# Seven block products for two chunks in every second round of an expert matmul, on one core

## The chip, the cores and the metric

The program runs on 1 core of one Trainium2 chip. The metric is the device time of one execution in microseconds (us); the kernel before has a median of 1713.93 us over 3 runs (1713.11 to 1713.99).

## The reference

Two transformer blocks in float32 on 256 tokens of width 1024. The part that matters is the PEER feed-forward of the first block: each token picks experts out of 16384, and the layer adds, for every picked expert e, g_e * gelu(u_e . x) * v_e:

```
u = expert_u[idx]
act = gelu(einsum('td,thkd->thk', xc, u))
w = (g * act)
return einsum('thk,thkd->td', w, expert_v[idx])
```

The kernel computes it densely. It holds W, the weight of every expert for every token (0 for those not picked), as `act_e` [128 experts, 128 chunks, 256 tokens], and multiplies it with all of `expert_v`, 16384 x 1024, in 128 chunks of 128 rows: out[token, d] = sum over chunks of W[chunk]^T x V[chunk].

## The kernel before

All weights stream through a ring of 4 slots (`RING`): `w_raw` (as loaded by SyncE's queue, 512 KB each), `w_hi` (rounded to the type TensorE takes, by ScalarE, line 1467) and `w_lo` (what rounding lost, by VectorE at line 2755 in this stage, by GpSimd at line 2024 in most others). The other operand is split likewise: `W_hi` by ScalarE (line 1703) and `W_lo` by VectorE (line 2720), 128 x 256 per chunk. A product of two float32 blocks is three matmuls: hi*hi, hi*lo, lo*hi (lines 652 to 654 in `row_chunk`).

In the expert_v stage a chunk gives 2 token tiles x 2 halves of d = 4 blocks of 128 x 512, so 12 matmuls into four PSUM banks `acc[0..3]`, which accumulate over all 128 chunks. The chunks go in 32 rounds of four (`v_round` on TensorE, ScalarE and VectorE, a hardware loop on each). The order on each engine is fixed by the code; the engines meet at semaphores: `hi0..3` and `lo0..3` (a slot's parts are ready), `used0..3` (TensorE is done with a slot), `W_hi` and `W_lo` (counts of chunks). `AHEAD` is 3: in round r ScalarE makes, in turn, `w_hi` of chunk 4r+3, `W_hi` of chunk 4r+2, `w_hi` of 4r+4, `W_hi` of 4r+3, and so on. So `W_hi` and `W_lo` of a round's third chunk, 4r+2, are made within that round, on both engines.

After the last round `residual("v", XB, ...)` on VectorE (line 2334) adds the four banks to `XB`, the residual stream read back from DRAM, and gives X; TensorE transposes X for the next projection (`zba`, weights `w_in_e`).

Of the kernel before, what the change touches and what calls it, by code (L numbers as in the profile page):

```python
# [28 lines left out]
F32 = mybir.dt.float32  # L29
# [218 lines left out]
def program(nc, ins, out):  # L248
    ctx = ExitStack()
    with ctx:  # L250
# [303 lines left out]
        @block.sync  # L554
        def _(sp):
            sp.dma_start(X[:, 0, :], x_dram[:, 0, :]).then_inc(sem("x0_in"), 16)
            sp.dma_start(cols[:, :], ins["cols"]).then_inc(sem("cols_in"), 16)

            def load(j, src=None, i=0):
                s = j % RING  # L560
                use = j // RING + i
                if j >= RING:

                    sp.wait_ge(sem(f"hi{s}"), upto(f"hi{s}", use))
                    sp.wait_ge(sem(f"lo{s}"), upto(f"lo{s}", use))
                width = PLAN[j][4]
                dst = w_raw[:, s, 0:width]
                if PLAN[j][1] == "pair":
                    dst = dst.rearrange("p (k c) -> p k c", k=2)
                sp.dma_start(dst, src_of(j) if src is None else src).then_inc(sem(f"raw{s}"), 16)  # L570

            j = 0
            while j < len(PLAN):
                if j == RING:
                    sp.dma_start(pos_i[:, :], ins["positions"]).then_inc(sem("pos_in"), 16)
                    sp.dma_start(rows_f[:, :], ins["freqs"].to_broadcast([P, N_FREQ])).then_inc(
                        sem("freq_in"), 16)
                if j == FIRST["query"] + 5:

                    sp.wait_ge(sem("ev_wout"), upto("ev_wout", 4))  # L580
                    sp.dma_start(KST[:, :, :], ins["sub_keys"]).then_inc(sem("keys_in"), 16)
                if j == FIRST["query"] + 8:

                    sp.wait_ge(sem("ev_wout"), upto("ev_wout", 4))
                    sp.dma_start(x_spill, X[:, :, :]).then_inc(sem("x_spilled"), 16)
                if j == FIRST["zba"]:

                    used(sp, V0 + 1)
                    sp.wait_ge(sem("x_spilled"), 16)
# [29 lines left out]
        def _(pe):  # L619
# [355 lines left out]
            def v_round(r, first=False, last=False):  # L975
                for q in range(4):
# [473 lines left out]
        def _(act):  # L1450
# [540 lines left out]
        def _(pool):  # L1991
# [35 lines left out]
            def block_masks():  # L2027

                pool.wait_ge(sem("gate"), STEPS)
                used(pool, V0 + 1)

                causal_mask(causal1, NEG)
                for c, base in ((0, 0), (1, P), (2, 0)):
                    g.iota(dist[:, c * P:(c + 1) * P], [[-1, P]], base=base, channel_multiplier=1,
                           allow_small_or_imprecise_dtypes=True).then_inc(sem("iota"), 1)
                then(g.memset(ones[:, :], 1.0), "ones")

                def within(m, size):  # L2040
# [147 lines left out]
            while j < len(PLAN):  # L2188
# [63 lines left out]
        def _(dve):  # L2252
# [998 lines left out]
```

## Time and profile before

| | |
|---|---|
| time of the profiled execution | 1715.6 us |
| its span (first to last instruction) | 1713.8 us |
| median of 3 runs | 1713.93 us |
| TensorE busy in the span | 1682.1 us, 98% |
| VectorE busy | 959.9 us, 56% |
| ScalarE busy | 901.9 us, 53% |
| GpSimd busy | 1023.8 us, 60% |
| mean granted TensorE clock | 0.995 |

Busy time is the time in which at least one instruction of the engine is in flight; for TensorE consecutive matmuls overlap, so the distance between starts, not the mean duration, tells the pace. The profiled execution took 1715.6 us, 1.8 us more than its span.

### The profile page before, as it was taken

The page shows a single profiled execution, that of the slowest core. Times are in us where ns is not written, and L with a number is a line of the kernel's source. Part 1 is how long each engine was busy: PE and PEld are TensorE (multiplying, and loading weights), DVE is VectorE, ACT ScalarE, POOL GpSimd, SP SyncE. Part 2 cuts the span into 40 slices and gives each one's busy share as a digit, 9 for nine tenths or more (in the row PEclk, how much of TensorE's full clock was granted, in tenths as well). Part 3 has the DMA queues.
Part 4 walks back from the last instruction along what each step waited for, and adds up shares of the span by engine and source line. Part 5 has one row for each costly group of instructions (what it writes and reads, how often), then busy time and mean ns, then how long its engine had stood idle before and what let it go on. Part 6 is the DMA issues. An engine that isn't in the chain of part 4 may idle for free.

```text
span 1713.8 us, 29468 instructions
## 1 busy us (share of the span) xinstructions
PE 1682.1 (98%) x9320; PEld 1438.1 (84%) x9320; DVE 959.9 (56%) x2062; ACT 901.9 (53%) x1638; POOL 1023.8 (60%) x549
## 2 busy tenths in 40 slices
PE   9999999999999999999999999999999999899998
PEld 7887998888888888888888888978888777788887
DVE  6233389887788875555555557753222366532222
ACT  5565644445554445544554466526455555555554
POOL 4846768888777762000000078528888885578887
PEclk9999999999999999999999999999999999999999
DMA  6633545555444446566556645115555554255553
GB/s 225 176 96 133 207 160 184 184 192 186 163 161 161 160 160 198 194 195 192 190 193 196 217 148 156 54 50 178 187 193 193 169 178 135 87 179 195 189 191 123
DMA packets 83074, 288.18 MB, mean 168 GB/s; under 512 B 9265, under 2 KB 9265, under 8 KB 82481
## 3 DMA queue, kind: packets, MB, share of 16 engines
q1 hardware_dynamic: 82560, 286.10, 51.5%
q8 instruction: 45, 0.74, 0.2%
q10 hardware_dynamic: 432, 1.05, 0.2%
q14 instruction: 37, 0.30, 0.1%
HBM read 285.01 MB, written 2.10 MB: 168 GB/s over the span
## 4 chain that ended last, share of the span: by engine, by line
PE 89%; DVE 3%; ACT 3%; POOL 3%; issue 2%; DMA 1%; DVEq 0%; ACTq 0%; POOLq 0%; SPq 0%
PE col L955 14%; PE acc L652 13%; PE acc L653 13%; PE acc L654 13%; PE col L959 7%; PE col L1251 7%; PE col L1255 4%; POOL w_lo L2024 2%; PE col L689 1%; PE col L690 1%; PE col L691 1%; PE mb L971 1%; PE mb L972 1%; PE acc L1170 1%; ACT w_hi L1467 1%
## 5 line engine op out<-in xcount | busy, mean ns | idle before, releaser
L2024 POOL TENSOR_TENSOR w_lo<-w_raw,w_hi 128x1024 fp32r<-128x1024 f32 (+1 forms) x403 | 953.3, 2381 | 291.5 <-ACT w_hi L1467 269.2
L1467 ACT ACTIVATE w_hi<-w_raw 128x1024 fp32r<-128x1024 f32 (+1 forms) x539 | 565.4, 1052 | 292.4 <-PE acc L654 230.1
L955 PE MATMUL col<-hT,w_hi 128*128 128x512 f32 x1024 | 259.2, 395 | 0.0
L955 PEld LDWEIGHTS col<-hT,w_hi 128*128 128x128 f32 x1024 | 183.8, 189 | 32.8
L652 PE MATMUL acc<-w_hi,W_hi 128*128 128x512 f32 x512 | 199.4, 389 | 0.4 <-ACT W_hi L1688 0.3
L654 PE MATMUL acc<-w_hi,W_lo 128*128 128x512 f32 x512 | 199.2, 389 | 0.0
L653 PE MATMUL acc<-w_lo,W_hi 128*128 128x512 f32 x512 | 199.2, 389 | 0.0
L2066 POOL TENSOR_SCALAR_AFFINE_SELECT WST<-WST 128x512 f32<-128x512 f32 x1 | 1.0, 955 | 319.5 <-DMA WST<-in_gmlp_w 319.5
L2755 DVE TENSOR_TENSOR w_lo<-w_raw,w_hi 128x1024 fp32r<-128x1024 f32 x128 | 156.2, 1221 | 1.2 <-ACT w_hi L1467 1.2
L959 PEld LDWEIGHTS col<-hT,w_lo 128*128 128x128 f32 x1024 | 139.7, 190 | 10.2
L3002 DVE TENSOR_REDUCE mb<-col 128x256 f32<-128x512 f32 x64 | 44.8, 700 | 180.4 <-PE col L1255 180.4
L959 PE MATMUL col<-hT,w_lo 128*128 128x256 f32 x1024 | 142.6, 282 | 0.0
L2720 DVE TENSOR_TENSOR W_lo<-act_e,W_hi 128x256 fp32r<-128x256 f32 x128 | 54.5, 426 | 146.4 <-ACT W_hi L1703 146.2
L1251 PE MATMUL col<-hT,w_hi 128*128 128x512 f32 x512 | 128.9, 392 | 1.8 <-DVE hT L2288 1.8
L652 PE MATMUL acc<-w_hi,hT 128*128 128x512 f32 (+2 forms) x304 | 117.2, 386 | 6.4 <-DVE w_lo L2354 2.3
L2539 DVE TENSOR_REDUCE acc<-col 128x256 f32<-128x512 f32 x128 | 89.5, 699 | 60.0 <-PE col L959 53.7
L653 PE MATMUL acc<-w_lo,hT 128*128 128x512 f32 (+2 forms) x304 | 116.4, 383 | 0.0
L1251 PEld LDWEIGHTS col<-hT,w_hi 128*128 128x128 f32 x512 | 95.9, 188 | 24.2 <-DVE hT L2288 2.5
L654 PE MATMUL acc<-w_hi,hT 128*128 128x512 f32 (+2 forms) x304 | 115.9, 382 | 0.0
L652 PEld LDWEIGHTS acc<-w_hi,W_hi 128*128 128x128 f32 x512 | 96.1, 188 | 20.8 <-DVE act_e L2714 0.6
L654 PEld LDWEIGHTS acc<-w_hi,W_lo 128*128 128x128 f32 x512 | 96.1, 188 | 20.2
L653 PEld LDWEIGHTS acc<-w_lo,W_hi 128*128 128x128 f32 x512 | 96.1, 188 | 19.8
(589 smaller groups left out, 3071.6 us busy)
## 6 DMA issues: line engine op xcount, KB each, us to landing
w_raw<-in_expert_u SPq DMA_DIRECT2D x128, 512.0 KB, 3.3
w_raw<-in_expert_v SPq DMA_DIRECT2D x128, 512.0 KB, 4.3
w_raw<-in_w_mlp SPq DMA_DIRECT2D x128, 512.0 KB, 3.4
w_raw<-in_w_in SPq DMA_DIRECT2D x24, 512.0 KB, 3.7
w_raw<-in_w_qkv_o SPq DMA_DIRECT2D x24, 512.0 KB, 4.2
w_raw<-in_w_query SPq DMA_DIRECT2D x16, 512.0 KB, 3.3
w_raw<-in_w_gate SPq DMA_DIRECT2D x16, 512.0 KB, 3.3
w_raw<-in_w_qkv_e SPq DMA_DIRECT2D x12, 512.0 KB, 3.9
```

What stands on the lines that cost most here:

```text
L652: mm(o, hi(t), w_hi[:, s, a:b], start=first, stop=False)
L653: mm(o, hi(t), w_lo[:, s, a:b], start=False, stop=False)
L654: m = mm(o, lo(t), w_hi[:, s, a:b], start=False, stop=last)
L955: mm(both, wh[:, k, :], hT[:, :, k, :], start=k == 0, stop=k == KD - 1, skip_group_check=True)
L959: m = mm(both[:, 0, :], wl[:, k, :], hT_hi[:, k, :], start=False, stop=k == KD - 1, skip_group_check=True)
L1251: mm(bank[:, :].rearrange("p (a s) -> p a s", a=2), wh[:, k, :], hT[:, :, k, :], start=k == 0, stop=k == KD - 1, skip_group_check=True)
L1255: m = mm(bank[:, 0:SEQ], wl[:, k, :], hT_hi[:, k, :], start=False, stop=k == KD - 1, skip_group_check=True)
L1467: f(w_hi[:, s, 0:w], w_raw[:, s, 0:w], ACT.Copy).then_inc(sem(f"hi{s}"), 1)
L2024: g.tensor_tensor(w_lo[:, s, 0:w], w_raw[:, s, 0:w], w_hi[:, s, 0:w].bitcast(F32), ALU.subtract).then_inc(sem(f"lo{s}"), 1)
L2539: v.tensor_reduce(sum_ps[n % 2], col[n % 2][:, :].rearrange("p (a s) -> p s a", a=2), AX_X, ALU.add).then_inc(sem("u_sum"), 1)
L2720: v.tensor_tensor(lo[:, q, :], act_e[:, c, :], hi[:, q, :].bitcast(F32), ALU.subtract).then_inc(sem("W_lo"), 1)
L2755: v.tensor_tensor(w_lo[:, s, :], w_raw[:, s, :], w_hi[:, s, :].bitcast(F32), ALU.subtract).then_inc(sem(f"lo{s}"), 1)
```

## The change

In rounds 6, 8, ..., 30 (13 rounds, `PAIRS_V`) the first two chunks are multiplied together. Let A11, A12, A21, A22 be the two chunks' W as blocks (token tile, chunk), 128 x 128 each, and B11, B12, B21, B22 their V as blocks (chunk, half of d), 128 x 512 each. `VS` holds A11-A21, A21-A22, (A21-A22)-A11 and that plus A12; `VT` holds B22+B12, B11+B12, (B11+B12)+B22 and that plus B21. Seven products (A11*B11, A12*B21, VS3*B22, VS1*VT1, VS0*VT0, VS2*VT2, A22*VT3, in this order in `v_pair`) then give the four output blocks that took 8. Each product is again three matmuls, so `v_pair` has 21 where two chunks had 24. Four of the seven results go to PSUM banks of their own (`col[0]`, `col[1]`, `mb[0]`, `mb[1]`), three to `acc`; the four are added to `XB` once, in `pair_sums` on VectorE, in the last round.

VectorE makes the sums (`block_sums`: 6 instructions) and the low parts of the sums, ScalarE the high parts (`next_pair`), both in the round ahead of the pair (`paired_round`). Of chunk 4r only the first half is split, and the two chunks' `W_hi` and `W_lo` are one instruction of 128 x 512 each. At the start of the round that begins with a pair, ScalarE waits for the semaphore `paired`, which TensorE raises with the last matmul of `v_pair`; the last use of `W_hi` slot 1 is in that product. SyncE loads rounds 7 to 31 by written-out instructions and not in its loop, waits for `t_sum` ahead of reloading slot 3 after a pair, for `T_lo` ahead of `XB`, and for `paired` ahead of `rows`. GpSimd's order stays as it is.

```diff
+PAIRED, UNPAIRED = 6, NKEYS // 4 - 1
+PAIRS_V = (UNPAIRED - PAIRED + 1) // 2
@@ SyncE
+                    sp.wait_ge(sem("T_lo"), 2 * PAIRS_V)
                     sp.wait_ge(sem("x_spilled"), 16)
                     sp.dma_start(XB[:, :, :], x_spill).then_inc(sem("x_back"), 16)
...
                     sp.wait_ge(sem("W_lo"), ROWS_OVER)
+                    sp.wait_ge(sem("paired"), PAIRS_V)
                     sp.dma_start(rows[:, :], ins["rows"].to_broadcast([P, R_ALL])).then_inc(
                         sem("rows_in"), 16)
@@ TensorE
+            def v_pair(r, m, first=False, last=False):
...
+                def product(o, hi, lo, b_hi, b_lo, begin=False, end=False):
+                    mm(o[:, :], hi, b_hi, start=begin, stop=False)
+                    mm(o[:, :], hi, b_lo, start=False, stop=False)
+                    return mm(o[:, :], lo, b_hi, start=False, stop=end)
...
+                product(col[0], W_hi[:, 0, 0:P], W_lo[:, 0, 0:P], w_hi[:, s0, a], w_lo[:, s0, a],
+                        first, last).then_inc(sem(f"used{s0}"), 1)
+                chunk_in(V0 + 1, r)
+                product(acc[0], W_hi[:, 1, 0:P], W_lo[:, 1, 0:P], w_hi[:, s1, a], w_lo[:, s1, a])
+                pe.wait_ge(sem("S_hi"), m + 1)
+                pe.wait_ge(sem("S_lo"), m + 1)
+                product(acc[1], VS_hi[:, 3, :], VS_lo[:, 3, :], w_hi[:, s1, b],
+                        w_lo[:, s1, b]).then_inc(sem(f"used{s1}"), 1)
+                for i, (o, n, t) in enumerate(((col[1], 1, 1), (mb[1], 0, 0), (mb[0], 2, 2))):
+                    if i % 2 == 0:
+                        pe.wait_ge(sem("T_hi"), m * 2 + 1 + i // 2)
+                        pe.wait_ge(sem("T_lo"), m * 2 + 1 + i // 2)
+                    product(o, VS_hi[:, n, :], VS_lo[:, n, :], VT_hi[:, t, :], VT_lo[:, t, :],
+                            first, last)
+                product(acc[2], W_hi[:, 1, P:2 * P], W_lo[:, 1, P:2 * P], VT_hi[:, 3, :],
+                        VT_lo[:, 3, :]).then_inc(sem("paired"), 1)
@@ ScalarE
+            def paired_round(r, m, first=False):
+                split(V0 + AHEAD, r)
+                gated_hi(r, 2)
+                gated_hi(r, 3)
+                next_pair(r, m, first)
+                split(V0 + 6, r)
...
+            paired_round(PAIRED - 1, 0, first=True)
+            with act.Fori(1, PAIRS_V) as m:
+                act.wait_ge(sem("paired"), m)
+                v_round(m * 2 + (PAIRED - 2))
+                paired_round(m * 2 + (PAIRED - 1), m)
+            act.wait_ge(sem("paired"), PAIRS_V)
+            v_round(UNPAIRED - 1)
+            v_round(UNPAIRED, count=2)
@@ VectorE
+            v_round(UNPAIRED - 1)
             for q in range(4):
                 if q < 2:
                     gated_lo(NKEYS - 2 + q, q + 2)
+                if q == 1:
+                    pair_sums()
                 weight_lo(V0 + q + AHEAD, NKEYS // 4 - 1)
-            dve.wait_ge(sem("x_back"), 16)
             residual("v", XB, 1.0 / GATE)
```

What the order of instructions shows at two places. First ScalarE, in the loop over rounds; slots 3, 0, 1 and 2 of the ring hold a round's first to fourth chunk. Before, the head of the loop over rounds:

```order
L1467 ACTIVATE w_hi<-w_raw 128x1024 [waits used2]
L1703 ISA [waits used1]
L1703 ACTIVATE W_hi<-act_e 128x256
L1467 ACTIVATE w_hi<-w_raw 128x1024 [waits used3,raw3]
L1703 ISA [waits used2]
```

Now the head of the loop over pairs of rounds, in the round that begins with a pair on TensorE:

```order
L1532 ISA [waits paired]
L570 REGISTER_ALU [waits raw2]
L1536 ACTIVATE w_hi<-w_raw 128x1024 [waits used2]
L1772 ISA [waits used1]
L1772 ACTIVATE W_hi<-act_e 128x256
L1536 ACTIVATE w_hi<-w_raw 128x1024 [waits used3,raw3]
```

The same instructions stand behind one more wait; the first `W_hi` there is that of the round's third chunk. On TensorE, the end of a pair and the head of that third chunk read now:

```order
L1007 MATMUL acc<-VT_hi,W_hi 128x512
L1008 MATMUL acc<-VT_lo,W_hi 128x512
L1009 MATMUL acc<-VT_hi,W_lo 128x512
L678 MATMUL acc<-w_hi,W_hi 128x512 [waits hi1,lo1,W_lo,W_hi]
L679 MATMUL acc<-w_lo,W_hi 128x512
```

So the third chunk, which waits for `W_hi` and `W_lo`, follows directly on the product that raises `paired`. The second place is VectorE in the last round. Before:

```order
L2720 TENSOR_TENSOR W_lo<-act_e,W_hi 128x256 [waits W_hi]
L2755 TENSOR_TENSOR w_lo<-w_raw,w_hi 128x1024 [waits used3,hi3]
L2755 TENSOR_TENSOR w_lo<-w_raw,w_hi 128x1024 [waits used0,hi0]
L2755 TENSOR_TENSOR w_lo<-w_raw,w_hi 128x1024 [waits used1,hi1]
L2334 SCALAR_TENSOR_TENSOR X<-acc,XB 128x512 [waits acc_full,x_back]
```

And now:

```order
L2828 TENSOR_TENSOR W_lo<-act_e,W_hi 128x256 [waits W_hi]
L2936 COPY VE<-col 128x512 [waits x_back,paired]
L2933 SCALAR_TENSOR_TENSOR XB<-col,XB 128x512 [waits dve]
L2938 TENSOR_TENSOR VE<-mb,VE 128x512 [waits dve]
L2933 SCALAR_TENSOR_TENSOR XB<-VE,XB 128x512 [waits dve]
L2933 SCALAR_TENSOR_TENSOR XB<-col,XB 128x512 [waits dve] x2
L2942 TENSOR_TENSOR VE<-mb,VE 128x512 [waits dve]
L2933 SCALAR_TENSOR_TENSOR XB<-VE,XB 128x512 [waits dve] x2
L2863 TENSOR_TENSOR w_lo<-w_raw,w_hi 128x1024 [waits used3,hi3,dve]
L2863 TENSOR_TENSOR w_lo<-w_raw,w_hi 128x1024 [waits used0,hi0]
L2863 TENSOR_TENSOR w_lo<-w_raw,w_hi 128x1024 [waits used1,hi1]
L2442 SCALAR_TENSOR_TENSOR X<-acc,XB 128x512 [waits acc_full] x3
```

Nine instructions of 128 x 512 now stand between the last chunk's `W_lo` and the three `w_lo` of the next projection, and so ahead of the residual.

## Rows read from the trace of the kernel before

**Rows 1.** The page: span, busy time of each engine
```profile
span 1713.8 us, 29468 instructions
PE 1682.1 (98%) x9320; PEld 1438.1 (84%) x9320; DVE 959.9 (56%) x2062; ACT 901.9 (53%) x1638; POOL 1023.8 (60%) x549
```

**Rows 2.** Windows: length, busy us (count) by engine, clock, DMA share, GB/s
```profile
636.00:985.00 349.00, 348.62 (x1538) 288.13 (x1536) 201.13 (x259) 175.65 (x257) 13.80 (x29) 1.00 0.60 196
```

**Rows 3.** Groups by line of 636 to 984: busy us, mean ns | idle before, releaser
```profile
L2755 DVE TENSOR_TENSOR w_lo<-w_raw,w_hi 128x1024 fp32r<-128x1024 f32 x128 | 156.2, 1221 | 1.2 <-ACT w_hi L1467 1.2
L1467 ACT ACTIVATE w_hi<-w_raw 128x1024 fp32r<-128x1024 f32 x129 | 136.8, 1061 | 171.9 <-PE acc L654 168.7 <-DMA w_raw<-in_w_in_e 2.6 <-DVE act_e L2714 0.5
L2720 DVE TENSOR_TENSOR W_lo<-act_e,W_hi 128x256 fp32r<-128x256 f32 x128 | 54.5, 426 | 146.4 <-ACT W_hi L1703 146.2 <-ACT W_hi L1688 0.2
```

**Rows 4.** Timeline of one chunk: start us, us, instruction [idle before <-releaser]
```profile
799.95 0.39 PE L654 MATMUL acc<-w_hi,W_lo 128*128 128x512 f32 x1
...
800.38 1.06 ACT L1467 ACTIVATE w_hi<-w_raw 128x1024 fp32r<-128x1024 f32 x1 [1.29 <-PE acc L654]
...
801.34 0.40 ACT L1703 ACTIVATE W_hi<-act_e 128x256 fp32r x1
...
801.90 0.43 DVE L2720 TENSOR_TENSOR W_lo<-act_e,W_hi 128x256 fp32r<-128x256 f32 x1 [1.12 <-ACT W_hi L1703]
...
802.24 1.22 DVE L2755 TENSOR_TENSOR w_lo<-w_raw,w_hi 128x1024 fp32r<-128x1024 f32 x1
...
802.67 0.39 PE L654 MATMUL acc<-w_hi,W_lo 128*128 128x512 f32 x1
```

**Rows 5.** Timeline at the stage's start, where TensorE waits for the first split
```profile
635.90 0.76 DVE L2720 TENSOR_TENSOR W_lo<-act_e,W_hi 128x256 fp32r<-128x256 f32 x2 [0.16 <-ACT W_hi L1688]
...
636.43 0.47 PE L652 MATMUL acc<-w_hi,W_hi 128*128 128x512 f32 x1 [0.26 <-ACT W_hi L1688]
```

**Rows 6.** Groups by line of the span: the sizes of the added work
```profile
L2497 DVE TENSOR_TENSOR M<-acc,M 128x512 f32<-128x512 f32 x4 | 2.6, 681 | 0.0
L2873 DVE COPY fT<-mb 128x512 f32<-128x512 f32 x4 | 2.8, 692 | 2.9 <-PE mb L1070 2.9
L2776 DVE SCALAR_TENSOR_TENSOR X<-X,rstd,rows 128x512 f32<-128x512 f32 x4 | 2.8, 746 | 0.8 <-POOL rstd L2080 0.8
L2904 DVE SCALAR_TENSOR_TENSOR OC<-mb,cols,UV 128x128 f32<-128x128 f32 x8 | 2.2, 344 | 0.0
L1512 ACT ACTIVATE hT<-mb 128x512 fp32r<-128x512 f32 x8 | 4.3, 595 | 13.7 <-PE mb L724 8.3 <-PE mb L828 5.4
```

**Rows 7.** Timeline of the last round and the residual, engine by engine
```profile
966.89 0.33 SPq L570 DMA_DIRECT2D w_raw<-in_expert_v  x1
967.48 0.33 SPq L590 DMA_DIRECT2D XB<-x_spill  x1
967.87 0.42 SPq L593 DMA_DIRECT2D WST<-in_gmlp_w  x1
968.34 0.42 SPq L596 DMA_DIRECT2D rows<-in_rows  x1
969.50 27.05 SPq L570 DMA_DIRECT2D w_raw<-in_w_in_e  x8
...
978.47 1.06 ACT L1467 ACTIVATE w_hi<-w_raw 128x1024 fp32r<-128x1024 f32 x1 [2.59 <-DMA w_raw<-in_w_in_e]
...
979.87 0.42 DVE L2720 TENSOR_TENSOR W_lo<-act_e,W_hi 128x256 fp32r<-128x256 f32 x1 [2.40 <-ACT W_hi L1703]
980.21 2.35 DVE L2755 TENSOR_TENSOR w_lo<-w_raw,w_hi 128x1024 fp32r<-128x1024 f32 x2
983.77 1.23 DVE L2755 TENSOR_TENSOR w_lo<-w_raw,w_hi 128x1024 fp32r<-128x1024 f32 x1 [1.20 <-ACT w_hi L1467]
984.91 2.48 DVE L2334 SCALAR_TENSOR_TENSOR X<-acc,XB 128x512 f32<-128x512 f32 x4
...
984.91 0.39 PE L654 MATMUL acc<-w_hi,W_lo 128*128 128x512 f32 x1
```

**Rows 8.** DMA issues of the stage: count, KB each, median us to landing
```profile
w_raw<-in_expert_v SPq DMA_DIRECT2D x119, 512.0 KB, 4.3
```

**Rows 9.** Idle of TensorE and its clock: timeline rows and windows
```profile
1151.13 0.66 PE L1222 MATMUL mb<-ident,OC 128*128 128x128 f32 x4 [1.77 <-DVE OC L2947]
...
9.87 0.58 PE L652 MATMUL acc<-w_hi,hT 128*128 128x512 f32 x1 [1.91 <-DVE w_lo L2354]
10.25 0.63 PE L653 MATMUL acc<-w_lo,hT 128*128 128x512 f32 x1
...
1150.00:1155.00 5.00, 3.87 (x19) 3.30 (x20) 2.87 (x6) 0.60 (x1) 0.39 (x1) 1.00 0.44 165
5.00:10.00 5.00, 3.08 (x19) 2.47 (x19) 2.38 (x4) 3.38 (x8) 0.00 (x0) 1.00 1.03 407
10.00:15.00 5.00, 5.00 (x16) 3.93 (x17) 4.44 (x8) 5.00 (x13) 1.00 (x2) 0.66 0.52 149
```

More of the change, by code:

```diff
@@ L392, in program @@
         rows = big("rows", 0, [P, R_ALL])
+        VT_hi = big("VT_hi", 0, [P, 4, 512], F32R)
+        VT_lo = big("VT_lo", 8, [P, 4, 512], F32R)
+        VS = big("VS", 16, [P, 4, P])
+        VS_hi = big("VS_hi", 18, [P, 4, P], F32R)
+        VS_lo = big("VS_lo", 20, [P, 4, P], F32R)
+        VE = big("VE", 16, [P, 512])
+        SUMS_OVER = 22
+        VT = at("VT", HT + 4 * KB, [P, 4, 512])
         hq_hi = big("hq_hi", 0, [P, KD, SEQ], F32R)
@@ L598, in _ @@
                 if j in LOOPS:
-                    with sp.Fori(0, LOOPS[j]) as i:
+                    looped = PAIRED + 1 if j == V0 else LOOPS[j]
+                    with sp.Fori(0, looped) as i:
                         for q in range(4):
@@ L605, in _ @@
                             load(j + q, src, i)
+                    for i in range(looped, LOOPS[j]):
+                        if (i - PAIRED) % 2:
+                            sp.wait_ge(sem("t_sum"), 3 * ((i - PAIRED) // 2 + 1))
+                        for q in range(4):
+                            load(j + 4 * i + q)
                     j += 4 * LOOPS[j]
@@ L973, in gates, with v_round @@
                 m.then_inc(sem("gate"), 1)
-            def v_round(r, first=False, last=False):
-                for q in range(4):
+            def v_pair(r, m, first=False, last=False):
+                s0, s1 = V0 % RING, (V0 + 1) % RING
+                a, b = slice(0, 512), slice(512, 1024)
+                def product(o, hi, lo, b_hi, b_lo, begin=False, end=False):
+                    mm(o[:, :], hi, b_hi, start=begin, stop=False)
+                    mm(o[:, :], hi, b_lo, start=False, stop=False)
+                    return mm(o[:, :], lo, b_hi, start=False, stop=end)
+                if first:
+                    pe.wait_ge(sem("u_sum"), NKEYS)
+                    pe.wait_ge(sem("gated"), STEPS)
+                    pe.wait_ge(sem("gate_kept"), STEPS)
+                pe.wait_ge(sem("W_hi"), r * 4 + 2)
+                pe.wait_ge(sem("W_lo"), r * 4 + 2)
+                chunk_in(V0, r)
+                product(col[0], W_hi[:, 0, 0:P], W_lo[:, 0, 0:P], w_hi[:, s0, a], w_lo[:, s0, a],
[14 more added lines that the diff above has]
+                        VT_lo[:, 3, :]).then_inc(sem("paired"), 1)
+            def v_round(r, first=False, last=False, chunks=range(4)):
+                for q in chunks:
                     n = r * 4 + q
@@ L1015, in _ @@
             v_round(0, first=True)
-            with pe.Fori(1, NKEYS // 4 - 1) as r:
+            with pe.Fori(1, PAIRED) as r:
                 v_round(r)
-            v_round(NKEYS // 4 - 1, last=True)
+            v_pair(PAIRED, 0, first=True)
+            v_round(PAIRED, chunks=(2, 3))
+            v_round(PAIRED + 1)
+            with pe.Fori(1, PAIRS_V - 1) as m:
+                v_pair(m * 2 + PAIRED, m)
+                v_round(m * 2 + PAIRED, chunks=(2, 3))
+                v_round(m * 2 + (PAIRED + 1))
+            v_pair(UNPAIRED - 1, PAIRS_V - 1, last=True)
+            v_round(UNPAIRED - 1, chunks=(2, 3))
+            v_round(UNPAIRED, last=True)
             raw_T(T_EVEN, "ev_v")
@@ L1710, in v_round, with next_pair @@
                         gated_hi(r, q + 2)
+            def next_pair(r, m, first=False):
+                j, s = V0 + 4, V0 % RING
+                act.wait_ge(sem(f"raw{s}"), upto(f"raw{s}", (j // RING + 1 + r) * 16))
+                used(act, j - RING, r)
+                f(w_hi[:, s, 0:512], w_raw[:, s, 0:512], ACT.Copy).then_inc(sem(f"hi{s}"), 1)
+                split(j + 1, r)
+                if first:
+                    used(act, V0 + 1, r)
+                    act.wait_ge(sem("W_lo"), SUMS_OVER)
+                else:
+                    act.wait_ge(sem("paired"), m)
+                f(W_hi[:, 0:2, :], act_e[:, bass.ds(r * 4 + 4, 2), :], ACT.Copy).then_inc(
+                    sem("W_hi"), 2)
+                act.wait_ge(sem("s_sum"), m * 3 + 3)
+                f(VS_hi[:, :, :], VS[:, :, :], ACT.Copy).then_inc(sem("S_hi"), 1)
+                for i in range(2):
+                    act.wait_ge(sem("t_sum"), m * 3 + 1 + 2 * i)
+                    f(VT_hi[:, 2 * i:2 * i + 2, :], VT[:, 2 * i:2 * i + 2, :], ACT.Copy).then_inc(
+                        sem("T_hi"), 1)
+            def paired_round(r, m, first=False):
[4 more added lines that the diff above has]
+                split(V0 + 6, r)
             act.wait_ge(sem("u_gated"), STEPS)
             v_round(0)
-            with act.Fori(1, NKEYS // 4 - 1) as r:
+            with act.Fori(1, PAIRED - 1) as r:
                 v_round(r)
-            v_round(NKEYS // 4 - 1, count=2)
+            paired_round(PAIRED - 1, 0, first=True)
+            with act.Fori(1, PAIRS_V) as m:
+                act.wait_ge(sem("paired"), m)
+                v_round(m * 2 + (PAIRED - 2))
[3 more added lines that the diff above has]
+            v_round(UNPAIRED, count=2)
             done[0] = FIRST["zba"] + AHEAD
@@ L2063, in block_masks, with gmlp_weights @@
                      "masks")
+            def gmlp_weights():
                 pool.wait_ge(sem("wst_in"), 16)
@@ L2209, in _ @@
                     block_masks()
+                    gmlp_weights()
                     j = FIRST["zba"] + AHEAD
@@ L2756, in weight_lo, with v_round @@
                                 ALU.subtract).then_inc(sem(f"lo{s}"), 1)
-            with dve.Fori(0, NKEYS // 4 - 1) as r:
+            def v_round(r):
                 for q in range(4):
@@ new lines, in paired_round @@
+            def paired_round(r, m, first=False):
+                gated_lo(r * 4 + 2, 2)
+                weight_lo(V0 + AHEAD, r)
+                gated_lo(r * 4 + 3, 3)
+                block_sums(r, m, first)
+                j, s = V0 + 4, V0 % RING
+                dve.wait_ge(sem(f"hi{s}"), upto(f"hi{s}", j // RING + 1 + r))
+                used(dve, j - RING, r)
+                v.tensor_tensor(w_lo[:, s, 0:512], w_raw[:, s, 0:512], w_hi[:, s, 0:512].bitcast(F32),
+                                ALU.subtract).then_inc(sem(f"lo{s}"), 1)
+                weight_lo(j + 1, r)
+                dve.wait_ge(sem("W_hi"), r * 4 + 6)
+                v.tensor_tensor(W_lo[:, 0:2, :], act_e[:, bass.ds(r * 4 + 4, 2), :],
+                                W_hi[:, 0:2, :].bitcast(F32), ALU.subtract).then_inc(sem("W_lo"), 2)
+                dve.wait_ge(sem("S_hi"), m + 1)
+                v.tensor_tensor(VS_lo[:, :, :], VS[:, :, :], VS_hi[:, :, :].bitcast(F32),
+                                ALU.subtract).then_inc(sem("S_lo"), 1)
+                for i in range(2):
+                    dve.wait_ge(sem("T_hi"), m * 2 + 1 + i)
+                    n = slice(2 * i, 2 * i + 2)
+                    v.tensor_tensor(VT_lo[:, n, :], VT[:, n, :], VT_hi[:, n, :].bitcast(F32),
+                                    ALU.subtract).then_inc(sem("T_lo"), 1)
+                weight_lo(V0 + 6, r)
@@ new lines, in pair_sums, with add @@
+            def pair_sums():
+                dve.wait_ge(sem("paired"), PAIRS_V)
+                dve.wait_ge(sem("x_back"), 16)
+                def add(src, t, n, sign):
+                    c = slice(n * 512, (n + 1) * 512)
+                    then(v.scalar_tensor_tensor(out=XB[:, t, c], in0=src[:, :], scalar=sign / GATE,
+                                                in1=XB[:, t, c], op0=ALU.mult, op1=ALU.add))
+                then(v.tensor_copy(VE[:, :], col[0][:, :]))
+                add(col[0], 0, 0, 1.0)
+                then(v.tensor_tensor(VE[:, :], mb[0][:, :], VE[:, :], ALU.add))
+                add(VE, 0, 1, -1.0)
+                add(col[1], 0, 1, 1.0)
+                add(col[1], 1, 1, 1.0)
+                then(v.tensor_tensor(VE[:, :], mb[1][:, :], VE[:, :], ALU.add))
+                add(VE, 1, 0, 1.0)
+                add(VE, 1, 1, -1.0)
@@ L2762, in _ @@
+            with dve.Fori(0, PAIRED - 1) as r:
+                v_round(r)
+            paired_round(PAIRED - 1, 0, first=True)
+            with dve.Fori(1, PAIRS_V) as m:
+                v_round(m * 2 + (PAIRED - 2))
+                paired_round(m * 2 + (PAIRED - 1), m)
+            v_round(UNPAIRED - 1)
             for q in range(4):
```

28 lines of the change are left out of this document (added).

## The prediction

> **What bounds the kernel now.** I read the page's busy times first, then the windows of the expert_v stage, its groups by line, and last the timelines of one chunk and of the stage's end. TensorE is busy for 1682.1 of 1713.8 us [rows 1], and in the window that holds the expert_v stage, 636 to 985 us, for 348.62 of 349.00 us at a granted clock of 1.00, the 2.4 GHz level [rows 2]. VectorE has 201.13 us of work there, ScalarE 175.65, GpSimd 13.80, and the DMA engines are 60% busy [rows 2]. So TensorE alone sets the pace: one matmul started at 799.95 us and the one at the same place in the next chunk at 802.67 [rows 4], 2.72 us for 12 matmuls, 0.2267 us each. ScalarE's idle time in the stage is 168.7 us of waiting for TensorE to free a slot, and VectorE's is 146.2 us of waiting for ScalarE's `W_hi` [rows 3]. None of that costs time as long as both finish ahead of TensorE.
>
> **The change, part by part.**
>
> *Matmuls removed.* 13 pairs lose 3 matmuls each: 39 x 0.2267 = 8.8 us saved. The matmuls of the products have the size of those they replace, so I take the same pace for them.
>
> *A new wait behind each pair, the term that decides.* The order shows that ScalarE, at the head of each round that begins with a pair, now waits for `paired`, the last matmul of the pair. Behind that wait stand, in order, `w_hi` of the round's fourth chunk and `W_hi` of its third; VectorE makes `W_lo` from that; and TensorE's next matmul needs both. None of these exists when the pair ends. Before, ScalarE waited there only for a slot freed at the end of the previous round, so all of it lay beside the round's first two chunks. The chain is read from one chunk [rows 4]: last matmul starts at 799.95, ScalarE is released at 800.38 (0.43 later), its `W_hi` starts at 801.34 (0.96 behind the `w_hi`), VectorE's `W_lo` at 801.90 and ends 0.43 later, 802.33. From there to TensorE: where it waited for such splits at the stage's start, the first `W_lo` ended near 635.90 + 0.43 = 636.33 (duration from [rows 3]) and the matmul started at 636.43, 0.10 later, and took 0.47 in place of 0.39 [rows 5], 0.08 more. So from last matmul to next start: 802.33 + 0.10 - 799.95 = 2.48 us where 0.23 was, plus 0.08: 2.33 us lost per pair, 13 x 2.33 = 30.3 us. Bounds: without the 0.08, and with no latency but the durations, 0.39 + 0.96 + 0.40 + 0.43 - 0.23 = 1.95 us (25 us in all); with 0.2 us more for wake-ups and a later release, 2.6 us (34 us in all). I take 30.3. In this idle time, 2.1 us a pair, everything else catches up, but nothing uses it.
>
> *Work added to VectorE and ScalarE.* In the round ahead of a pair VectorE makes, with durations of the nearest rows: 3 full `w_lo` and the two `VT_lo`, and the first `VT` sum, all 128 x 1024, 6 x 1.22; two `W_lo` and the first `VS` sum, 128 x 256, 3 x 0.43 [rows 3]; two `VT` sums, the half `w_lo`, the joint `W_lo` and `VS_lo`, 128 x 512, 5 x 0.68, and two `VS` sums of 128 x 128, 2 x 0.34 [rows 6]. That is 7.3 + 1.3 + 3.4 + 0.7 = 12.7 us, against 4 x (1.22 + 0.43) = 6.6 before: more than the 10.88 us of the round, yet 19.3 us per two rounds, where TensorE will take 93 x 0.2267 + 2.33 = 23.4. The order in the round matters more. With the round's start as 0, VectorE begins at about 1.8 (ScalarE's `w_hi` 1.06 and `W_hi` 0.40 come first), ends the sums at 7.1, has slot 3 and slot 0 and the joint `W_lo` done at about 9.5, `VS_lo` at 10.1, the `VT_lo` at 11.3 and 12.5. TensorE wants them at 10.9 (pair's start), 10.88 + 6 x 0.2267 = 12.2, 10.88 + 9 x 0.2267 = 12.9 and 14.3. Margins of 1.4 to 2.1 us: cost nothing. If one operation of the chain took double (1.2 us more, the `VT` sum with its broadcast operand is unlike any row) it still fits; two such would cost about 1 us a pair, 13 us. None of them can gain. ScalarE has 3 x 1.06 + 2 x 1.06 + 2 x 0.40 + 3 x 0.60 = 7.9 us in that round and is in time.
>
> *Loads.* SyncE's loads follow the `lo` of their slot. After a stall three slots come free 1.4 us apart, and a chunk lands 4.3 us after issue [rows 8]; the tightest is the fourth chunk of the next round, which lands about when ScalarE asks for it (7.6 us after the pair). Up to half a microsecond late is inside the margins above: nothing, with 0 to 0.3 us a pair (4 us) kept for the range.
>
> *The end of the stage.* Before, the last round starts at 984.91 - 47 x 0.2267 = 974.26 us and the residual at 984.91, 10.65 us into it, on the heels of VectorE's last `w_lo` and overlapping the last matmul [rows 7]. Two things move. First, SyncE issues the load of the last chunk when `w_lo` of a chunk 4 back is done; in round 30 that one now lies behind the pair. It was issued at 966.89, 7.4 us ahead of the last round; now (pair's end at 5.0 in a round of 45 x 0.2267 + 2.33 = 12.5 us, and 3.3 us on) 4.2 us ahead. The four issues behind it move too, so `w_hi` of the first zba chunk, which began at 978.47 as its data landed, 4.2 us into the last round [rows 7], begins at about 7.4. The last chunk's `W_hi` stands behind it: done at 8.7, its `W_lo` at 9.3, while TensorE wants it at 36 x 0.2267 = 8.2: a further 1.3 us of idle. Second, the nine instructions of `pair_sums` begin at 9.3 and each waits for the one before: six read PSUM (a copy, two sums, three additions to `XB`) at 0.69 and three read SBUF alone at 0.75 [rows 6], 6.4 us, to 15.7. Behind them come three `w_lo` back to back, 1.14 apart as two of them are in 2.35 us now [rows 7]: 19.1. The residual starts there, not at 10.65: 8.5 us later, and TensorE stands idle from 12.2 on. Behind the residual all goes on as before (transposes, `hT`, zba). Bounds: if the later loads cost nothing, the sums start where `W_lo` ended before, at about 6.0, and the residual at 15.9, 5.3 us later; with 0.15 us more for each wait of an instruction on the one before, 10 us. I take 8.5.
>
> *Sum.* -8.8 + 30.3 + 8.5 = +30.0 us on the profiled execution's 1715.6 us: 1745.6; on the median of 1713.93 it is 1743.9. I forecast 1745 us.
>
> **The clock.** In this trace an idle time of 1.77 us within dense matmuls left the granted clock at 1.00 (1151.13, window 1150 to 1155), but one of 1.91 us behind small transposes was followed by matmuls 0.43 us apart at the 1.2 GHz level, window 10 to 15 at 0.66 [rows 9]: (1 - 0.66) x 5 us is 1.7 us lost. The new idle times, 2.1 us, are longer than both, amid dense matmuls as the first. The Trainium skill (TensorE: Matmul & The Clock Gate, HAM oscillation) tells of a kernel whose TensorE waited for DMA in every K-tile, and in which the restart at the lower clock was paid in each of them. By that rule the fall comes with every pair; by the row at 1151 it comes with none. That is a rival of its own:
>
> **Rivals.**
> - *The clock falls behind pairs.* For it: the idle time is longer than the one at 9.87 that ended in a fall. Against: the one at 1151. If it does so every time, 13 x 1.7 = 22 us on top: 1767; at one pair in three, 1753.
> - *Faster or level: the wait is hidden.* Place: ScalarE's wait for `paired`. It would cost nothing if `W_hi` of the third chunk did not depend on it. The price decides at 8.8 / 13 = 0.68 us a pair: below it the change gains in the rounds. Then -8.8 + 8.5 gives 1714, and with the last round's sums hidden as well, 1706. Against it: the order and [rows 4], which have 1.8 us of sheer work between release and `W_lo`'s end.
> - *VectorE becomes the bound.* The sums take double; two late operations cost 1 us a pair or more: 1758 to 1765. For it: VectorE has 12.7 us of work in a round of 10.9. Against: the 23.4 us of two rounds and margins of over 1.4 us.
>
> **How the numbers follow.** My forecast 0.65 (own range 1738 to 1751 from the bounds: -8.8 + 25 + 5.3 and -8.8 + 34 + 10), clock 0.18, VectorE 0.07, hidden wait 0.06 (half of it level, half faster), the rest 0.04 slower for reasons not seen. The range that holds 8 in 10 takes the forecast's own and the clock at up to one pair in two: 1737 to 1758. A measurement of this kernel can tell 0.2%, 3.4 us. Faster by more 0.04, within 0.03, slower 0.93.
>
> **What would show it.** TensorE idle of 2.0 to 2.3 us, 13 times, before the third chunk's first matmul, put down to VectorE's `W_lo` or ScalarE's `W_hi`; none before or within a pair; 39 fewer matmuls. ScalarE's idle time before `w_hi` at the loop's head ended by the pair's last product. Before the residual, nine VectorE instructions of 0.7 us and an idle TensorE for 6 to 7 us. The granted clock of the stage at 1.00 (below 0.97 would be the first rival). Wrong is the forecast if TensorE goes on without a gap behind a pair, if it waits within pairs for `VT_lo`, or if the stage's own time, 348.6 us before, grows by less than 15 us.

## The result: 2.15% slower, and where the profile after puts it

The kernel with the pairs takes 1750.71 us (median of 4 runs, 1748.98 to 1752.81); the kernel before, measured with it, 1713.77 us. The ratio is 1.0215, with a 95% interval of 1.0203 to 1.0227: 36.9 us slower where 31 us over the median before were forecast (1745). The profiled executions took 1750.57 and 1715.6 us, 35.0 apart. The page and the windows after, against [rows 1, 2]:

```profile
span 1748.8 us, 29212 instructions
PE 1682.2 (96%) x9281; PEld 1434.1 (82%) x9281; DVE 1029.7 (59%) x2175; ACT 922.7 (53%) x1664; POOL 1024.2 (59%) x549
...
0.00:636.00 636.00, 628.61 (x3972) 553.58 (x3972) 439.30 (x1177) 332.95 (x648) 463.08 (x227) 1.00 0.53 170
636.00:1022.00 386.00, 348.98 (x1499) 283.52 (x1499) 271.77 (x374) 196.18 (x284) 14.21 (x29) 0.98 0.54 177
```

There are 39 matmuls fewer (9320 to 9281), and none of it shows in the busy time: in the stage's window TensorE is busy for 349 us as before, in 386 us and at a mean clock of 0.98. By an estimate from the rows below, the lower clock behind pairs (4.7 us) and, at each of 13 waits, a last matmul that nothing overlaps and a longer first one (0.16 + 0.08 us) put back 7.8 of the 8.8 us. Up to 636 us nothing has changed (628.70 us busy before, at a clock of 1.00). The waits of TensorE over the span say what the new idle time is (engine, line, releaser: us in total, times, longest):

```profile
PE acc L678 <- ACT W_hi L1772: 29.0, 13, 2.3
PE col L724 <- DVE X L2442: 8.0, 2, 7.5
```

There are thirteen waits for the third chunk's `W_hi`, twelve of 2.25 us and the last of 1.96, and one wait of 7.5 us ahead of the transposes. The timeline behind one pair, to be read against [rows 4]:

```profile
802.53 0.39 PE L1009 MATMUL acc<-VT_hi,W_lo 128*128 128x512 f32 x1
803.12 1.06 ACT L1536 ACTIVATE w_hi<-w_raw 128x1024 fp32r<-128x1024 f32 x1 [5.36 <-PE acc L1009]
804.09 0.40 ACT L1772 ACTIVATE W_hi<-act_e 128x256 fp32r x1
...
804.64 0.42 DVE L2828 TENSOR_TENSOR W_lo<-act_e,W_hi 128x256 fp32r<-128x256 f32 x1 [4.42 <-ACT W_hi L1772]
...
805.17 0.77 PE L678 MATMUL acc<-w_hi,W_hi 128*128 128x512 f32 x1 [2.25 <-ACT W_hi L1772]
```

ScalarE stood for 5.36 us at its wait with the work of the third chunk behind it; once the pair's last product was done, `w_hi`, `W_hi` and `W_lo` followed one another with TensorE idle. 2.64 us lie between the two starts, where 0.23 is the pace. The first matmul takes 0.77 us here, where it takes 0.47 behind pairs without a fall: the clock had fallen. The starts of the third chunk after this pair, the one ahead and the one behind, with two windows around (length, busy by engine, granted clock, DMA share, GB/s):

```profile
781.59 0.47 PE L678 MATMUL acc<-w_hi,W_hi 128*128 128x512 f32 x1 [2.25 <-ACT W_hi L1772]
...
830.35 0.47 PE L678 MATMUL acc<-w_hi,W_hi 128*128 128x512 f32 x1 [2.25 <-ACT W_hi L1772]
853.96 0.47 PE L678 MATMUL acc<-w_hi,W_hi 128*128 128x512 f32 x1 [2.25 <-ACT W_hi L1772]
...
805.00:810.00 5.00, 4.83 (x14) 3.93 (x15) 4.15 (x6) 2.17 (x5) 0.00 (x0) 0.66 0.45 134
...
855.00:860.00 5.00, 5.00 (x24) 4.12 (x23) 4.36 (x6) 2.37 (x5) 0.00 (x0) 1.00 0.69 190
```

From 805.17 to 830.35 two rounds took 25.18 us, from 830.35 to 853.96 they took 23.61, for the same work. The difference, 1.57 us, is the price of the fall to the 1.2 GHz level. It came behind 3 of the 13 pairs (at 709, 805 and 925 us: the first, the fifth and the tenth). The end of the stage, against [rows 7]:

```profile
1009.04 1.06 ACT L1536 ACTIVATE w_hi<-w_raw 128x1024 fp32r<-128x1024 f32 x1 [5.01 <-DMA w_raw<-in_w_in_e]
...
1010.44 0.42 DVE L2828 TENSOR_TENSOR W_lo<-act_e,W_hi 128x256 fp32r<-128x256 f32 x1 [4.82 <-ACT W_hi L1772]
1010.78 0.68 DVE L2936 COPY VE<-col 128x512 f32<-128x512 f32 x1
...
1015.86 1.42 DVE L2933 SCALAR_TENSOR_TENSOR XB<-VE,XB 128x512 f32<-128x512 f32 x2
1017.31 3.50 DVE L2863 TENSOR_TENSOR w_lo<-w_raw,w_hi 128x1024 fp32r<-128x1024 f32 x3
1020.72 2.48 DVE L2442 SCALAR_TENSOR_TENSOR X<-acc,XB 128x512 f32<-128x512 f32 x4
...
1021.46 0.69 PE L724 MATMUL col<-ident,X 128*128 128x128 f32 x2 [7.49 <-DVE X L2442]
```

The nine sums take 1010.78 to 1017.28, 6.5 us, three `w_lo` another 3.4, and only then the residual starts.

The account, at the residual's start (984.91 us before, 1020.72 after: 35.8 us):

| term | forecast | measured |
|---|---|---|
| 39 matmuls fewer | -8.8 | -8.8 |
| waits behind pairs | 30.3 | 12 x 2.49 + 2.20 = 32.1 |
| lower clock behind pairs | 0 | 25.24 + 25.18 + 25.11 - 3 x 23.61 = 4.7 |
| end of the stage | 8.5 | 18.3 - 10.65 = 7.7 |
| sum | 30.0 | 35.7 |

A wait costs 2.64 - 0.23 + 0.08 = 2.49 us (0.08 for the first matmul, as the prediction had it); behind the last pair 2.35 us lie between the starts, which makes 2.20. The last round starts at 1002.4 us (996.87 + 0.08 + 24 x 0.2267) and the residual 18.3 us into it. Counted from the stage's first matmul (636.43 us before, 636.17 after) the residual is 36.1 us later, so the table leaves 0.4 us open; the distance of two rounds without a fall, 23.61 us against 93 x 0.2267 = 21.08, gives 2.53 for a wait and would close it. Behind the residual the span ends after 728.1 us where 728.9 were before: 35.0 us in all.

### The profile page after: what moved, and what is told of

The parts are those of the page before. It is cut to its first block, busy times and chain, and to the rows that moved or that the text cites. A ratio compares the mean times of both kernels' runs of the same rounds, so it can differ in the third digit from the quotient of the medians.

```text
span 1748.8 us, 29212 instructions
## 1 busy us (share of the span) xinstructions
PE 1682.2 (96%) x9281; PEld 1434.1 (82%) x9281; DVE 1029.7 (59%) x2175; ACT 922.7 (53%) x1664; POOL 1024.2 (59%) x549
## 4 chain that ended last, share of the span: by engine, by line
PE 88%; DVE 4%; ACT 3%; issue 2%; POOL 2%; DMA 1%; ACTq 0%; DVEq 0%; POOLq 0%; SPq 0%
PE col L981 13%; PE acc L678 12%; PE acc L679 12%; PE acc L680 12%; PE col L985 7%; PE col L1320 7%; PE col L1324 3%; PE col L715 1%; PE col L716 1%; PE col L717 1%; PE mb L997 1%; PE mb L998 1%; POOL w_lo L2129 1%; PE acc L1239 1%; PE mb L750 1%
## 5 line engine op out<-in xcount | busy, mean ns | idle before, releaser
L1536 ACT ACTIVATE w_hi<-w_raw 128x1024 fp32r<-128x1024 f32 (+2 forms) x526 | 550.8, 1050 | 286.4 <-PE acc L680 157.1
L678 PE MATMUL acc<-w_hi,W_hi 128*128 128x512 f32 x408 | 162.3, 398 | 29.6 <-ACT W_hi L1772 29.0
L679 PE MATMUL acc<-w_lo,W_hi 128*128 128x512 f32 x408 | 160.6, 394 | 0.0
L680 PE MATMUL acc<-w_hi,W_lo 128*128 128x512 f32 x408 | 160.6, 394 | 0.0
L2863 DVE TENSOR_TENSOR w_lo<-w_raw,w_hi 128x1024 fp32r<-128x1024 f32 x115 | 140.2, 1220 | 0.0
L678 PEld LDWEIGHTS acc<-w_hi,W_hi 128*128 128x128 f32 x408 | 77.8, 191 | 51.6 <-ACT W_hi L1772 34.7
L2828 DVE TENSOR_TENSOR W_lo<-act_e,W_hi 128x256 fp32r<-128x256 f32 x102 | 43.0, 423 | 113.7 <-ACT W_hi L1772 113.5
L1980 ACT ACTIVATE H_r<-mb 128x256 f32<-128x256 f32 x64 | 24.7, 385 | 154.3 <-DVE mb L3194 154.3
L678 PE MATMUL acc<-w_hi,H_hi 128*128 128x512 f32 x256 | 100.7, 393 | 0.0
```

The lines of the kernel that those rows point to most:

```text
L678: mm(o, hi(t), w_hi[:, s, a:b], start=first, stop=False)
L679: mm(o, hi(t), w_lo[:, s, a:b], start=False, stop=False)
L680: m = mm(o, lo(t), w_hi[:, s, a:b], start=False, stop=last)
L1536: f(w_hi[:, s, 0:w], w_raw[:, s, 0:w], ACT.Copy).then_inc(sem(f"hi{s}"), 1)
```

## The experiments

### The wait moved to the instruction that needs it

```diff
-            def v_round(r, count=4):
+            def v_round(r, count=4, pairs=None):
                 for q in range(4):
                     split(V0 + q + AHEAD, r)
+                    if q == 3 and pairs is not None:
+                        act.wait_ge(sem("paired"), pairs)
                     if q < count:
                         gated_hi(r, q + 2)
...
-                act.wait_ge(sem("paired"), m)
-                v_round(m * 2 + (PAIRED - 2))
+                v_round(m * 2 + (PAIRED - 2), pairs=m)
```

> The changed kernel with ScalarE's wait for `paired` moved from the head of the paired round to ahead of the one instruction that needs it, W_hi of slot 1 of the next round. Theory (the wait's place costs 2.2 us behind each of 13 pairs, and part of these idle times makes the clock fall): the 13 gaps of 2 us in front of the third chunk are gone, the granted clock of the stage is 1.00, and the time falls by 29 us of waits and some 5 us of lower clock, from 1750.7 to about 1716 us; what is left over the kernel before is the last round. Rival (VectorE's added work is what holds TensorE back, and only shows as a wait for W_hi because it comes last): the gaps shrink by less than half and TensorE waits for VT_lo or W_lo within the pairs; time 1730 us or more.

Measured: 1713.61 us, ratio to the kernel before 1.0007 (0.9998 to 1.0017). In a later set of runs on the same chip (expectation there: 

> e1_late_wait once more, to compare it with e5 on the same chip: 1713.6 us, level with the kernel before.

) it took 1712.27 us, ratio 0.9991 (0.9982 to 1.0001). The place of one wait is worth 37 us. TensorE's wait at the stage's end, and a window over twelve pairs:

```profile
PE col L724 <- DVE X L2442: 7.2, 2, 6.7
...
700.00:950.00 250.00, 250.00 (x1105) 207.01 (x1104) 204.46 (x285) 147.00 (x213) 0.00 (x0) 1.00 0.61 201
```

250 us of 250 busy at a clock of 1.00: no wait before, within or behind a pair, with VectorE at 204 us of work. The rival, VectorE as the bound, is refuted. The kernel is level, and not 8.8 us faster, because of the end of the stage: the residual starts at 982.13 us, only 2.8 us earlier than before. TensorE's last matmul ended 6.7 us before the first transpose, and the clock is low there:

```profile
982.13 2.47 DVE L2442 SCALAR_TENSOR_TENSOR X<-acc,XB 128x512 f32<-128x512 f32 x4
...
981.00:986.00 5.00, 2.62 (x11) 2.23 (x12) 3.86 (x7) 2.53 (x7) 0.98 (x3) 0.50 0.54 158
986.00:991.00 5.00, 5.00 (x22) 4.43 (x21) 4.42 (x10) 4.42 (x12) 1.34 (x3) 0.64 0.00 0
```

Of these 2.8 us the medians show nothing in the first set of runs (0.2 us slower) and 2.0 in the second. The executions of this kernel have mean granted clocks of 0.990 to 0.995, those of the kernel before 0.995 to 0.998.

### One instruction less in the waited-for chain

```diff
                 for q in range(4):
+                    if w_first and q == 0:
+                        gated_hi(r, q + 2)
                     split(V0 + q + AHEAD, r)
-                    if q < count:
+                    if q < count and not (w_first and q == 0):
                         gated_hi(r, q + 2)
```

(the wait stays at the round's head, `w_first` is set in the rounds behind it)

> The changed kernel with the wait left at the head of the paired round, but with W_hi of the third chunk ahead of w_hi of the fourth behind it. Theory: only the chain release, W_hi, W_lo is left between the pair and the third chunk, so each of the 13 idle times of 2.0 us shrinks by the 0.96 us that w_hi took there, to 1.0 us; 12.5 us less, and with idle times this short the clock no longer falls, 5 us less: 1733 us. Rival (the clock falls for reasons other than the length of the gap): 12.5 us less only, 1738 us, with stretches of the clock at 0.7 left.

Measured: 1739.65 us, 1.0149 (1.0132 to 1.0166). The starts of the third chunk, and windows around the first:

```profile
708.31 0.47 PE L678 MATMUL acc<-w_hi,W_hi 128*128 128x512 f32 x1 [1.36 <-ACT W_hi L1772]
731.03 0.47 PE L678 MATMUL acc<-w_hi,W_hi 128*128 128x512 f32 x1 [1.36 <-ACT W_hi L1772]
...
706.00:711.00 5.00, 3.64 (x17) 2.70 (x16) 2.68 (x4) 3.79 (x6) 0.00 (x0) 1.00 0.21 72
711.00:716.00 5.00, 5.00 (x24) 4.14 (x23) 3.82 (x7) 3.13 (x6) 0.00 (x0) 1.00 0.84 275
```

The idle time fell from 2.25 to 1.36 us, by 0.89 (1.01 us are left behind the last pair), and the granted clock of the stage stayed at 1.00 behind all 13. The residual starts at 1005.26 us, 15.5 earlier than in the changed kernel, near the 17.5 expected: 13 x 0.89 and the 4.7 of lower clock, less 0.9 because TensorE waits 1.12 us for the last chunk's `W_hi` (995.51 us), where 0.24 was. But the median is 11 us lower, not 17.5: in this profile a later stretch gives 5 us back, behind a wait of 1.51 us for GpSimd's `w_lo` in the next projection, with the clock at 0.83, 0.50 and 0.64 in the windows from 1021 to 1036:

```profile
1022.78 0.47 PE L678 MATMUL acc<-w_hi,hT 128*128 128x512 f32 x1 [1.51 <-POOL w_lo L2131]
...
1026.00:1031.00 5.00, 5.00 (x18) 4.23 (x17) 0.00 (x0) 2.69 (x3) 4.31 (x3) 0.50 0.85 297
```

So the expectation failed in its sum and held in the place that it spoke of. By its number the measurement is nearer to the rival's 1738 us, but the rival's low clock behind pairs is not there. One profile shows that later stretch. Three executions took 1739.11 to 1740.49 us at a mean clock of 0.992 and the fourth 1735.09 at 0.994, which would fit a stretch that comes in most and not in all.

### One instruction more in it

The same edit with `W_hi` of the third chunk behind two `w_hi` in place of one (`gated_hi(r, 2)` in the turn of q = 1).

> The changed kernel with W_hi of the third chunk one instruction later behind the wait (after w_hi of the fourth and of the fifth chunk). Theory (the wait's chain is what TensorE waits for, and a longer idle time makes a fall of the clock more likely): each of the 13 idle times grows by 0.95 to 1.25 us, to 3.2 to 3.5, which is 12 to 16 us, and the clock falls behind more than 3 of the 13 pairs, each for 1.7 us: 1750.7 + 14 + 5 to 15 = 1770 to 1780 us. Rival (whether the clock falls depends on when the idle time comes, not on its length beyond 2 us): 1763 to 1767 us with 2 to 4 falls.

Measured: 1786.97 us, 1.0426 (1.0410 to 1.0443), 7 us above the range expected. The profiled execution is the longest of the four, 1793.58 us.

```profile
710.17 0.77 PE L678 MATMUL acc<-w_hi,W_hi 128*128 128x512 f32 x1 [3.20 <-ACT W_hi L1772]
737.60 0.77 PE L678 MATMUL acc<-w_hi,W_hi 128*128 128x512 f32 x1 [3.20 <-ACT W_hi L1772]
...
706.00:711.00 5.00, 1.80 (x7) 1.24 (x6) 1.36 (x2) 3.82 (x6) 0.00 (x0) 0.85 0.16 66
711.00:716.00 5.00, 5.00 (x13) 3.85 (x13) 3.14 (x5) 0.32 (x2) 0.00 (x0) 0.50 0.68 189
```

TensorE is idle for 3.20 us (2.90 behind the last pair), and behind each of the 13 pairs the first matmul takes 0.77 us. Two rounds take 27.3 us: 23.6 + 0.95 for the longer wait, so 2.8 us for the lower clock, more than the 1.57 above. The clock is low for longer: the windows from 706 to 721 us have 0.85, 0.50 and 0.97, which makes 6.8 us at the lower level, where those from 705 to 715 in the changed kernel have 0.96 and 0.70, which makes 3.4. The rival, that length has no part in it, is refuted: in the profiles, idle times amid dense matmuls of 1.36 us made the clock fall behind 0 of 12 pairs, of 2.25 us behind 3 of 12, of 3.20 us behind 12 of 12 (and those behind the last pair, 1.01, 1.96 and 2.90 us, behind none, none and one). The 12 are not 12 independent trials, as the pairs follow one another at an even 27.3 us. Nor does each execution look like the profile: the other three took 1786.37 to 1787.51 us at a mean clock of 0.973 to 0.974 against 0.969, 6 to 7 us less, which would fit two or three falls fewer at 2.8 us each. The Trainium skill (TensorE: Matmul & The Clock Gate, HAM oscillation) has a kernel that pays a restart at the lower clock with every K-tile; the profiles here agree with that for the longest of the three idle times only, 3.20 us.

### The nine sums left out

```diff
                 if q == 1:
-                    pair_sums()
+                    dve.wait_ge(sem("paired"), PAIRS_V)
+                    dve.wait_ge(sem("x_back"), 16)
```

> The changed kernel without the nine instructions of pair_sums (the four banks of the pairs are not added to the output, which leaves that part of the computation out); the waits for paired and x_back stay. Theory (the sums stand on the path from the last matmul to the residual): the residual starts 6.4 us earlier, the idle time of 7.5 us of TensorE ahead of the transposes shrinks to under 2, and with it the lower clock behind it goes (2 us): 1742 us. Rival (the late load of the next projection's weights sets the end of the stage): under 2 us less.

Measured: 1742.84 us, 1.0184 (1.0162 to 1.0206), 7.9 us less than the changed kernel. VectorE's end of the stage and the transposes:

```profile
1011.87 3.49 DVE L2863 TENSOR_TENSOR w_lo<-w_raw,w_hi 128x1024 fp32r<-128x1024 f32 x3
1015.28 1.88 DVE L2442 SCALAR_TENSOR_TENSOR X<-acc,XB 128x512 f32<-128x512 f32 x3
...
1016.02 0.44 PE L724 MATMUL col<-ident,X 128*128 128x128 f32 x2 [0.98 <-DVE X L2442]
```

This kernel leaves out adding the pairs' four banks to the output. The sums stood on the path: 0.98 us of idle time where it was 7.49, and the residual, counted from the stage's first matmul (637.25 us here), starts 378.0 us into the stage in place of 384.6. Behind the pairs its waits are the same, 29.0 us in 13, and the clock fell behind 3 of them too, but at other pairs (the second, the seventh and the twelfth, at 734, 853 and 973 us). The rounds' code is the same in both kernels, so it does not fix which pair is hit. The falls are evenly spaced all the same: 4 and 5 pairs apart in the changed kernel, 5 and 5 here. No run shows what sets this distance.

### Seven pairs in place of thirteen

```diff
-PAIRED, UNPAIRED = 6, NKEYS // 4 - 1
+PAIRED, UNPAIRED = 18, NKEYS // 4 - 1
```

> The changed kernel with pairs from round 18 on only, 7 in place of 13. Theory (each pair costs 2.2 us of waiting less 0.68 us of matmuls, and the end of the stage a fixed 8 us): 6 x 1.5 = 9 us less, and 2 us of lower clock less: 1739 us, so that the line through 7 and 13 pairs meets 0 pairs some 8 us above the kernel before. Rival (the cost is in the structure, code written out or loops, and not in the pairs): less than 3 us less.

Measured: 1738.26 us, 1.0154 (1.0133 to 1.0175), 12.5 us less than with 13 pairs, 2.1 us for each pair left out. That is 2.49 - 0.68 = 1.8 and a share of the clock, which fell behind 1 of the 7 pairs in the profile. The line through 13 and 7 pairs meets 0 pairs at 1723.7, 10 us above the kernel before. Of these, 7.7 are the end of the stage, in this profile again with 7.5 us of idle time ahead of the transposes; the rest is less than the spread of the kernel's own executions (1736.17 to 1743.40). The rival (code structure) is refuted.

### The pairs with the end of the stage rearranged

On top of the moved wait:

```diff
 # SyncE: XB ahead of the load of chunk 126
+                            if i == LOOPS[j] - 1 and q == 2:
+                                used(sp, V0 + 1)
+                                sp.wait_ge(sem("T_lo"), 2 * PAIRS_V)
+                                sp.wait_ge(sem("x_spilled"), 16)
+                                sp.dma_start(XB[:, :, :], x_spill).then_inc(sem("x_back"), 16)
 # ScalarE, last round
-            v_round(UNPAIRED, count=2)
+            split(V0 + AHEAD, UNPAIRED)
+            gated_hi(UNPAIRED, 2)
+            gated_hi(UNPAIRED, 3)
+            for q in range(1, 4):
+                split(V0 + q + AHEAD, UNPAIRED)
 # VectorE: pair_sums as a generator of 2, 2 and 5 instructions, advanced
 # behind the third and fourth w_lo of round 30 and the last W_lo of round 31
```

> e1_late_wait with the end of the stage rearranged: XB is loaded two chunks earlier, the nine instructions of pair_sums are spread over VectorE's idle times of rounds 30 and 31 (two in each of two places of round 30, five in round 31 while VectorE waits for the next projection's weights), and ScalarE makes the last chunk's W_hi ahead of w_hi of the next projection. Theory (in e1 the pairs' 8.8 us are won in the rounds and lost again at the end, where the residual starts 6 us after the last matmul): TensorE's idle time of 6.7 us ahead of the transposes falls below 1, the lower clock behind it goes, and the time is 8 us below e1: 1705 us, 0.5% faster than the kernel before. Rival (the residual waits for the late weights of the next projection, whoever makes the sums): 2 us below e1 or less.

Measured: 1704.87 us, ratio to the kernel before 0.9947 (0.9933 to 0.9962), 7.4 us below the moved wait alone in the same set of runs. This version beats both kernels. The rival, 2 us or less, is refuted. The three moves (the load of `XB`, the sums, the order of `W_hi`) were made together, so their shares are not shown.

```profile
636.00:978.00 342.00, 340.65 (x1502) 281.13 (x1500) 270.79 (x374) 196.93 (x287) 14.34 (x29) 1.00 0.61 201
...
976.65 2.47 DVE L2446 SCALAR_TENSOR_TENSOR X<-acc,XB 128x512 f32<-128x512 f32 x4
```

The residual starts 8.3 us earlier than in the kernel before (984.91), close to the 8.8 us of matmuls, and TensorE waits for it 1.6 us in two parts (1.1 before). The rest of the 9.4 us between the medians lies behind the residual, where the profile of the kernel before has two stretches at the lower clock (1440 to 1447 and 1468 to 1474 us) and this one has one (1453 to 1460). Between executions of the same granted clock, 0.997 or 0.998, the two kernels are 8.0 to 9.7 us apart (1703.11 to 1705.20 against 1712.84 to 1713.57), about the 8.8 of the matmuls.

## Why the prediction was right, step by step

**The decisive wait** was right in place, in what stood behind it and nearly in size. 13 waits put down to `W_hi`, none within a pair, and with the wait moved all of them gone. The forecast 2.33 us per pair measured 2.49: ScalarE started 0.59 us after the last matmul's start (802.53 to 803.12), not the 0.43 of [rows 4]; there its wait is an instruction of its own at the loop's head, with another behind it. Behind the last pair, where the trace has the wait on `w_hi` itself, it was 0.43 (994.52 to 994.95), and the loss 2.20.

**The matmuls saved** were worth what the pace of [rows 4] says: with the wait moved, the last products of the first and the thirteenth pair start at 706.5 and 959.5 us, 21.08 us for each two rounds, which is 93 x 0.2267 where 96 took 21.76.

**The end of the stage** was 7.7 us, not 8.5. The sums took 6.5 us as worked out (6.4). The zba weights were later by less: `w_hi` began 6.6 us into the last round, not 7.4, so TensorE's wait for the last chunk was 0.4 us and not 1.3.

**VectorE's added work** cost nothing, as worked out from its margins; the run with the moved wait shows it. The `VT` sum with its broadcast operand, for which no row of before existed, took 1.22 us as any other of its size:

```profile
L2885 DVE TENSOR_TENSOR VT<-w_raw 128x1024 f32<-128x1024 f32 x13 | 15.8, 1218 | 0.0
L2892 DVE TENSOR_TENSOR VT<-VT,w_raw 128x512 f32<-128x512 f32 x13 | 8.9, 683 | 0.0
```

**The clock** was the step that was mis-sized: the forecast took 0, from the one row of 1.77 us within dense matmuls, and kept falls as a rival at 0.18. They came behind 3 of 13 pairs, at 1.6 us each, near the rival's "one pair in three", and the stage's clock of 0.98 lies between the forecast's sign (1.00) and the rival's (below 0.97). With 4.7 us for it and 1.8 for the longer waits less 0.8 at the end, the sum of 30.0 becomes 35.7. It should have stood in the forecast itself with a share: the idle time foreseen was longer than any in the trace before that had left the clock alone.

**The range** held, but barely where it is the forecast's own: 1750.7 us lies at the top of "1738 to 1751". The bounds as written (-8.8 + 25 + 5.3 and -8.8 + 34 + 10) give 1735 to 1749 on the median and 1737 to 1751 on the profiled execution, so the measured median lies above the first of these. The rival of the hidden wait had the right prices for kernels that were not this one: it put 1714 us for the wait hidden and 1706 with the sums hidden as well, and the moved wait measured 1713.61 and the rearranged end 1704.87.

## What to carry to other kernels

Where a change puts a wait on an engine that works in order, read what is queued behind it and whether the waited-for engine needs that next; put the wait directly ahead of the one instruction that needs it. Here that one line decided between 2.15% slower and level. Look also at what a saving in a loop leaves to be gathered at its end: with the nine short instructions ahead of the residual, and a lower clock behind them, at most 2 of the 8.8 us were left in the medians until the end was rearranged.

## What the runs showed of the hardware

The same idle time of 2.25 us amid dense matmuls was followed by a fall of TensorE's clock in 3 of 12 cases in each of two profiles, at different pairs but evenly spaced, and in 1 of 6 in a third; 1.36 us in none of 12; 3.20 us in all 12, at 2.8 us each in place of 1.6. In another place of one profile (the kernel with one instruction less) 1.51 us was followed by a fall. A single idle time in a trace that left the clock alone says little of one half a microsecond longer that comes 13 times.
